# Second block: output transposes amid the branch product, heads ahead of the weight splits, gate sigmoids grouped, and a second pair of filling banks

## The chip, the cores and the metric

The kernel runs on one core of one Trainium2 chip. The metric is the device time of one execution in microseconds; lower is better. The engines named below are TensorE (PE in the profile: matmuls and transposes), VectorE (DVE), ScalarE (ACT), GpSimd (POOL) and SyncE (SP, which issues nearly all DMAs). All of them run at once, each through its own instruction stream in order, and they wait for one another on semaphores.

## The reference, cut to what matters

A first block (a hybrid of a state-space mixer and attention, a mixture of experts, a gated side input) is followed by a second one on the same 256 rows of 1024 numbers. The change touches the second block only:

```python
h = rms_norm_2(x, g_norm)
proj = h @ w_in
hy_in, z_hy, c_q, c_kv, k_rope, z_attn, gate_hy, gate_attn = split(proj)
u = short_conv(hy_in, w_short, b_short);  v_h, x1, x2 = split(u, 3)
zc = v_h
for o, gate in enumerate((x1, x2)):              # two rounds through spectra
    zc = gate * long_conv(zc, k_spec[:, o], hy_bias[o])
u_hy = (zc * silu(z_hy)) @ w_hy_out              # "branch", weights whn
q, k, v_a = ...                                  # from c_q, c_kv, k_rope: 8 heads
attn = dense_bidirectional_attention(q, k, v_a)
u_attn = (attn * silu(z_attn)) @ w_attn_out      # weights wa2
g_hy, g_at = split(sigmoid(concat([gate_hy, gate_attn]) + b_gate))
x = x + (g_hy * u_hy + g_at * u_attn) @ w_out    # weights wo2
```

## The kernel before

**Large products.** Every float32 weight is cut by columns and rows into tiles of at most 128x2048 numbers (four chunks of 128 rows by 512 columns). A tile passes through three stations: SP fetches it into one of four raw buffers; ACT writes its rounded high part (`weights` in `scalar`, L1209: `WH<-raw`); DVE writes the rest (`weights` in `vector`, L1705: `WL<-raw,WH`). High and low parts live in three slots, so a tile can be split only when the tile three before it has been used up by PE. The activations are split in the same way after their transposes: `high` on ACT (L1227) and `low` on DVE (L1735). A chunk of a product is then three matmuls for each half of the rows (`mul3`, L500), six in all, into two PSUM banks.

**Order of the tiles at the end.** The columns of z_attn ("za", two tiles), four gate groups (`("gate", 0)` to `("gate", 3)`, two tiles each), `whn` 0 and 1 (one tile each), `wa2` 0 and 1 (one each), `wo2` 0 and 1 (two each, called a and b below). 0 and 1 are the left and right 512 output columns.

**Filling.** The products that nobody needs at once are a list of single chunks, `todo`. Each engine's code calls `fill(n)` at the same places, which takes the next n chunks: PE multiplies; ACT and DVE (`filled`) split the weights that have come due and, behind a product's last chunk, take the product out of PSUM. za is taken out by ACT with a Silu, the gates by DVE with scale and bias (L1758), and then ACT applies the Sigmoid in place (L1271). The branch products (`whn` 0 and 1) are multiplied by the gates on DVE (L1766).

**PSUM banks.** `Ring` hands out the eight banks. `take` returns the next one of `ring.of` and first makes PE wait until the bank's former content has been taken out (its "drainer"). In the spectral stage `ring.of` is banks 0 to 5, and every filling product sits in banks 6 and 7.

**The stage with the spectra** (PE from 673.98 us on, `for o_ in range(2)` in `tensor`): two rounds of four forward products (`uf`, plain float32 from the arena), fillings (9 chunks in the first round, 4 and 3 in the second), two inverse products (`ui`), and more fillings (4 and 2). The eight za chunks and the sixteen of gates 0 and 1 are filled in here. Just ahead of it stand the products of the latents, `kq` and `kv`; the last bank of `kv` is taken out by ACT (L1618 and L1620).

**The stage with the heads** (PE from 739.02 us to 791 us): eleven steps. Each may hold a head's transposes (L509 from the arena), a chunk of filling, the scores of the head before, another chunk, the transposes of the exponentials (L509 from XN), and the product with the values, which is collected in banks 4 and 5. On ACT a step holds the copies of the transposed head (L1661, L1662), the exponentials (L1670), and for odd steps a copy of the weights (L1241); on DVE the row maxima (L2533, L2536) and for even steps that copy (L1745). Of the 24 filling chunks (gate 2, gate 3, branch 0, branch 1), 20 are used in the steps and the four of branch 1 behind them.

**The end.** DVE divides the heads' output by the sums and multiplies by silu(z_attn) (L2551, L2554, L2558, twice), PE transposes it (`transposed("o2T", ...)`, L509 from rt_), ACT and DVE split it, and `wa2` 0 and 1, the merge with the gates (L2566, L2569) and `wo2` 0 and 1 follow. The last step is `residual` on DVE (L2068) and the stores.

Of the kernel before, what the change touches and what calls it, by code (L numbers as in the profile page):

```python
# [14 lines left out]
ACT = mybir.ActivationFunctionType  # L15
# [150 lines left out]
def program(nc, A, out):  # L166
    ctx = ExitStack()
    with ctx:
# [326 lines left out]
        def tensor(e):  # L495
# [31 lines left out]

            open_fill = {}

            def fill(n):  # L530
                for name, c in todo.next(n):
                    key, lhs, ready, drainer, turned = fill_of[name]
                    if c == 0:
                        open_fill[name] = [ring.take((name, t), drainer, at=6 + t) for t in range(2)]
                    gemm_chunk(name, key, c, open_fill[name], lhs, ready, turned)
# [542 lines left out]
            todo.add(("gate", 0), 8)  # L1078
            todo.add(("gate", 1), 8)
            for o_ in range(2):  # L1080
                for f in range(2):
# [34 lines left out]
            todo.add(("branch", 1), 4)  # L1116
            ring.of = range(4)
            held_o2 = [ring.take(("o2", t), ve, at=4 + t) for t in range(2)]
# [34 lines left out]
            for h in range(11):  # L1153
# [9 lines left out]
                if h >= 3:  # L1163
                    values2(h - 3)
            fill(99)
            ring.of, ring.i = range(8), 0


            ve.wait_ge(e, "o2")
            transposed("o2T", lambda t: O2[:, t, :], 4)  # L1170
            gemm(("wa2", 0), ("wa2", 0), OT2, "o2T", (ve, ve))
# [24 lines left out]
        def scalar(e):  # L1196
# [42 lines left out]
            def drain_t(name, dst):  # L1239
                mm.wait_ge(e, name)  # L1240
                e.activation(dst, pb(name)[:, 0:dst.shape[1]], ACT.Copy).then_inc(ac.sem, ac.mark(name))  # L1241

            def filled(name, c):
                key = fill_of[name][0]
# [20 lines left out]
                elif name == "za":  # L1265
                    drain(name, ZA, ACT.Silu, by=rg)
                elif name[0] == "gate":
                    for t in range(2):
                        gv = G_[i // 2][:, t, (i % 2) * 512:(i % 2) * 512 + 512]
                        ve.wait_ge(e, (name, t))  # L1270
                        e.activation(gv, gv, ACT.Sigmoid).then_inc(ac.sem, ac.mark((name, t)))  # L1271
                weights(used(key))
# [402 lines left out]
            for h in range(11):  # L1675
# [7 lines left out]
                if 2 <= h <= 9 and h % 2:  # L1683
                    if h >= 6:
                        mm.wait_ge(e, ("pv2", h - 6))
                    drain_t(("p2", h - 2), P2[(h - 2) % 4])
            fill(99)
            high("o2T", OT2, 4, after=(("gate", 3), 1))
            weights(used(("wa2", 0)))
# [7 lines left out]
        def vector(e):  # L1697
# [48 lines left out]

            def filled(name, c):
                key = fill_of[name][0]
# [11 lines left out]
                elif name[0] == "branch":  # L1760
                    i = name[1]
                    ac.wait_ge(e, (("gate", i), 1))
                    for t in range(2):
                        gv = G1[:, t, 512 * i:512 * i + 512]
                        mm.wait_ge(e, (name, t))
                        e.tensor_tensor(gv, pb((name, t))[:, :], gv, ALU.mult).then_inc(ve.sem, ve.mark((name, t)))  # L1766
                weights(used(key))

            def fill(n):
                for name, c in todo.next(n):  # L1770
                    filled(name, c)

# [765 lines left out]
            for h in range(11):  # L2538
                fill(1)
                if 1 <= h <= 8:  # L2540
# [8 lines left out]
            for t in range(2):  # L2549
# [7 lines left out]
                ve.wait_ge(e, ("o2", t))  # L2557
                e.tensor_tensor(O2[:, t, :], O2[:, t, :], ZA[:, t, :], ALU.mult).then_inc(ve.sem, own("o2"))  # L2558
            fill(99)
            low("o2T", OT2, 4)  # L2560
            for i in range(2):
# [12 lines left out]
            low("m2T", HT, 8, first=4)  # L2574
            weights(used(("wa2", 1)))
            ac.wait_ge(e, "x 1")
            for i in range(2):
                residual(("wo2", i), i, ("x 2", i))
                weights(used(("wo2", i)))

# [159 lines left out]
```

## Time and profile before

| | us |
|---|---|
| median of 3 runs | 846.97 (846.54 to 847.56) |
| the profiled execution, its own time | 844.72 |
| its span from first to last instruction | 842.9 |
| PE busy in the span | 760.5 (90%) |
| DVE busy | 459.2 (54%) |
| ACT busy | 325.0 (39%) |

The span is what the views of the trace count in; 1.8 us lie around it. The median of the timed runs is 2.25 us above the profiled execution's own time. A row of the timeline gives the start, the duration and, in brackets, how long the engine had been idle before it and which instruction of which engine released it. Starts of neighbouring matmuls are more telling than durations, since matmuls overlap in the pipeline.

### The profile page before, as it was taken

To read this page: it belongs to the slowest core of one execution; us is meant where nothing else is said; L and a number is where in the kernel's file an instruction comes from. 1 tells how busy PE (TensorE), PEld (TensorE's weight loads), DVE (VectorE), ACT (ScalarE), POOL (GpSimd) and SP (SyncE) were. 2 spreads that over 40 slices of the span, in tenths; PEclk is the share of its full clock that TensorE was granted. 3 is DMA by queue.
4 is the path that set the end of the run, shared out by engine and by line. 5 is a ranking of instruction groups with operands and counts; after the bars stand their busy time and mean duration, and the time that the engine had idled before them with its cause. 6 is when DMAs were issued, how large, how long until landed. Compare 5 with 4: busy or idle time off the path is not lost.

```text
span 842.9 us, 11017 instructions
## 1 busy us (share of the span) xinstructions
PE 760.5 (90%) x4618; PEld 573.6 (68%) x4618; DVE 459.2 (54%) x813; ACT 325.0 (39%) x482; POOL 17.8 (2%) x14
## 2 busy tenths in 40 slices
PE   4999999999999997988799896779999999999898
PEld 4978877788778875555445542337999865678676
DVE  5778955547756755132142121028687786754653
ACT  5555446535464423111011010037755541267521
POOL 0000000000000000000000000001100020000000
PEclk9999999999999997999899898789999999999999
DMA  9555543333467596699999999875463734243301
GB/s 317 172 199 199 200 150 101 100 101 101 149 244 277 191 425 260 213 422 420 421 421 420 419 422 391 338 265 185 146 228 94 255 130 149 101 150 100 100 1 51
DMA packets 62578, 190.25 MB, mean 226 GB/s; under 512 B 7417, under 2 KB 11771, under 8 KB 50044
## 3 DMA queue, kind: packets, MB, share of 16 engines
q1 hardware_dynamic: 60750, 184.70, 58.6%
q10 hardware_dynamic: 1774, 4.79, 1.8%
q8 instruction: 38, 0.62, 0.3%
q14 instruction: 16, 0.13, 0.0%
HBM read 188.43 MB, written 1.05 MB: 225 GB/s over the span
## 4 chain that ended last, share of the span: by engine, by line
PE 59%; DMA 16%; DVE 13%; ACT 8%; issue 2%; POOL 1%; SPq 0%; ACTq 0%; DVEq 0%; POOLq 0%
PE pb L500 56%; DMA raw<-in_w_exp_up 7%; DVE WL L1705 4%; DMA WHo<-in_w_exp_up 4%; ACT WH L1209 4%; PE pb L509 3%; DMA WLo<-in_w_exp_up 3%; DMA raw<-in_w_exp_gate 2%; ACT arena L1365 1%; DMA X<-in_x 1%; DVE cv_ L1811 1%; DVE arena L1970 1%; POOL small L2587 1%; ACT arena L1237 0%; DVE arena L2016 0%
## 5 line engine op out<-in xcount | busy, mean ns | idle before, releaser
L1705 DVE TENSOR_TENSOR WL<-raw,WH 128x2048 fp32r<-128x2048 f32 (+5 forms) x80 | 173.4, 2177 | 98.2 <-ACT WH L1209 98.1
L1209 ACT ACTIVATE WH<-raw 128x2048 fp32r<-128x2048 f32 (+5 forms) x80 | 144.9, 1822 | 99.4 <-PE pb L500 89.9
L500 PE MATMUL pb<-WH,HTh 128*128 128x512 f32 (+2 forms) x384 | 156.0, 406 | 13.6 <-DVE HTl L1735 3.4
L500 PE MATMUL pb<-WL,HTh 128*128 128x512 f32 (+2 forms) x384 | 148.3, 386 | 0.0
L500 PE MATMUL pb<-WH,HTl 128*128 128x512 f32 (+2 forms) x384 | 148.0, 386 | 0.0
L500 PEld LDWEIGHTS pb<-WH,HTh 128*128 128x128 f32 x384 | 72.7, 189 | 33.7 <-DVE WL L1705 6.4
L500 PEld LDWEIGHTS pb<-WL,HTh 128*128 128x128 f32 x384 | 72.5, 189 | 14.4
L500 PEld LDWEIGHTS pb<-WH,HTl 128*128 128x128 f32 x384 | 72.8, 190 | 12.9 <-issue 1.0
L500 PE MATMUL pb<-arena 128*32 128x256 f32 (+6 forms) x268 | 64.0, 466 | 7.4 <-DMA arena<-in_w_exp_up 4.8
L500 PE MATMUL pb<-WH,arenao 128*128 128x512 f32 x192 | 59.6, 392 | 1.2 <-DVE arenao L1739 1.2
L2244 DVE TENSOR_TENSOR rt_<-rt_,pb 128x256 f32<-128x256 f32 x8 | 3.4, 421 | 98.9 <-ACT rt_ L1480 98.9
L500 PE MATMUL pb<-HTh,WH 128*128 128x256 f32 (+1 forms) x184 | 52.9, 287 | 0.1
L500 PE MATMUL pb<-HTh,WL 128*128 128x256 f32 (+1 forms) x184 | 52.4, 285 | 0.0
L500 PE MATMUL pb<-HTl,WH 128*128 128x256 f32 (+1 forms) x184 | 52.4, 285 | 0.0
L500 PE MATMUL pb<-raw,arena 128*32 128x256 f32 x272 | 37.7, 496 | 13.6 <-DMA raw<-in_w_exp_gate 6.9
L500 PEld LDWEIGHTS pb<-arena 128*32 128x32 f32 (+4 forms) x268 | 29.5, 168 | 28.2 <-issue 10.4
L1480 ACT ACTIVATE rt_<-pb 128x256 f32<-128x256 f32 x8 | 3.1, 383 | 105.3 <-PE pb L500 105.3
L500 PEld LDWEIGHTS pb<-WH,arenao 128*128 128x128 f32 x192 | 35.7, 188 | 8.6 <-DVE WL L1705 1.4
L500 PE MATMUL pb<-XN,arena 128*128 128x64 f32 (+2 forms) x144 | 37.9, 418 | 0.8 <-DVE arena L2016 0.8
L500 PE MATMUL pb<-WL,arenao 128*128 128x512 f32 x96 | 37.5, 390 | 0.0
L500 PEld LDWEIGHTS pb<-raw,arena 128*32 128x32 f32 x272 | 16.6, 141 | 28.5 <-DMA raw<-in_w_exp_gate 9.3
L500 PEld LDWEIGHTS pb<-HTh,WH 128*128 128x128 f32 (+1 forms) x184 | 35.0, 190 | 0.8 <-DVE WL L1705 0.5
(360 smaller groups left out, 1287.4 us busy)
## 6 DMA issues: line engine op xcount, KB each, us to landing
raw<-in_w_in SPq DMA_DIRECT2D x46, 1024.0 KB, 5.1
raw<-in_w_exp_up SPq DMA_DIRECT2D x16, 1024.0 KB, 21.3
arena<-in_w_exp_gate SPq DMA_DIRECT2D x14, 1024.0 KB, 19.1
WLo<-in_w_exp_down SPq DMA_DIRECT2D x11, 1024.0 KB, 17.0
raw<-in_w_exp_gate SPq DMA_DIRECT2D x10, 1024.0 KB, 14.8
WHo<-in_w_exp_down SPq DMA_DIRECT2D x9, 1024.0 KB, 16.5
raw<-in_w_out SPq DMA_DIRECT2D x8, 1024.0 KB, 5.1
arena<-in_w_exp_down SPq DMA_DIRECT2D x8, 1024.0 KB, 16.0
```

The source lines that it names most:

```text
L500: return e.matmul(o, l, r, start=start, stop=stop, skip_group_check=True)
L509: return e.transpose(o, i, ident[0:k, 0:k])
L1209: e.activation(h_, r_, ACT.Copy).then_inc(hi.sem, hi.mark(k))
L1365: ins = e.activation(S1[s][:, cut], S1[s][:, cut], ACT.Exp, bias=nmx[:, s, t:t + 1], scale=-1.0, accum_out=ssum[:, t, h:h + 1])
L1480: e.activation(HG[q % 2], pb(("gu", q))[:, 0:256], ACT.Silu).then_inc(ac.sem, ac.mark(("su", q)))
L1705: e.tensor_tensor(l_, r_, h_.bitcast(F32), ALU.subtract).then_inc(lo.sem, lo.mark(k))
L1811: e.scalar_tensor_tensor(out=cv[:, s:L], in0=u[:, 0:L - s], scalar=cw[:, 3 - s, g:g + 1], in1=cv[:, s:L], op0=ALU.mult, op1=ALU.add).then_inc(
L1970: ins = e.scalar_tensor_tensor(out=LM[:, h, :], in0=pb(("lm", t, h0))[:, (h - h0) * 128:(h - h0) * 128 + 128], scalar=Ac[:, t, h:h + 1], i ...
L2244: e.tensor_tensor(HG[q % 2], HG[q % 2], pb(("gu", q))[:, 256:512], ALU.mult).then_inc(ve.sem, ve.mark(("gu", q)))
L2587: e.tensor_tensor(ss, ss, half, ALU.pow).then_inc(po.sem, po.mark(("rs", n)))
```

## The change

Five edits, all in the second block:

1. In the spectral stage `ring.of` becomes banks 0 to 3, begun again at bank 0. The filling products alternate between banks 6 and 7 and banks 4 and 5. Behind the stage they are back at 6 and 7 alone.
2. ACT applies the sigmoid of gates 2 and 3 behind the last step of the heads, no longer behind each gate's last chunk, and splits `o2T` ahead of the last filling.
3. PE waits for the heads' output and transposes it behind the second of branch 1's four chunks, no longer behind the fourth.
4. DVE leaves out the split that comes due behind branch 0's last chunk until the heads' output is normalised, and writes the low part of `o2T` ahead of the last filling.
5. DVE splits the last tile (`wo2` 1 b) ahead of the residual of the left columns.

```diff
@@ tensor
-            open_fill = {}
+            open_fill, fill_at = {}, deque([6])
                     if c == 0:
-                        open_fill[name] = [ring.take((name, t), drainer, at=6 + t) for t in range(2)]
+                        open_fill[name] = [ring.take((name, t), drainer, at=fill_at[0] + t) for t in range(2)]
+                        fill_at.rotate(1)
...
             todo.add(("gate", 1), 8)
+            ring.of, ring.i = range(4), 0
+            fill_at.append(4)
             for o_ in range(2):
...
             todo.add(("branch", 1), 4)
-            ring.of = range(4)
+            fill_at.clear()
+            fill_at.append(6)
...
                 if h >= 3:
                     values2(h - 3)
+            fill(2)
+            ve.wait_ge(e, "o2")
+            transposed("o2T", lambda t: O2[:, t, :], 4)
             fill(99)
             ring.of, ring.i = range(8), 0
-            ve.wait_ge(e, "o2")
-            transposed("o2T", lambda t: O2[:, t, :], 4)
             gemm(("wa2", 0), ("wa2", 0), OT2, "o2T", (ve, ve))
@@ scalar
+            def sigmoid(i):
+                for t in range(2):
+                    gv = G_[i // 2][:, t, (i % 2) * 512:(i % 2) * 512 + 512]
+                    ve.wait_ge(e, (("gate", i), t))
+                    e.activation(gv, gv, ACT.Sigmoid).then_inc(ac.sem, ac.mark((("gate", i), t)))
...
-                elif name[0] == "gate":
-                    for t in range(2):
-                        gv = G_[i // 2][:, t, (i % 2) * 512:(i % 2) * 512 + 512]
-                        ve.wait_ge(e, (name, t))
-                        e.activation(gv, gv, ACT.Sigmoid).then_inc(ac.sem, ac.mark((name, t)))
+                elif name[0] == "gate" and i < 2:
+                    sigmoid(i)
                 weights(used(key))
...
+            for i in (2, 3):
+                sigmoid(i)
+            high("o2T", OT2, 4, after=(("gate", 3), 1))
             fill(99)
-            high("o2T", OT2, 4, after=(("gate", 3), 1))
             weights(used(("wa2", 0)))
@@ vector
-            def filled(name, c):
+            def filled(name, c, split):
...
-                weights(used(key))
-            def fill(n):
+                if split:
+                    weights(used(key))
+            def fill(n, split=True):
                 for name, c in todo.next(n):
-                    filled(name, c)
+                    filled(name, c, split)
...
             for h in range(11):
-                fill(1)
+                fill(1, h < 10)
...
                 e.tensor_tensor(O2[:, t, :], O2[:, t, :], ZA[:, t, :], ALU.mult).then_inc(ve.sem, own("o2"))
+            weights(used(("whn", 0)))
+            low("o2T", OT2, 4)
             fill(99)
-            low("o2T", OT2, 4)
...
             weights(used(("wa2", 1)))
+            weights(used(("wo2", 0)))
             ac.wait_ge(e, "x 1")
             for i in range(2):
                 residual(("wo2", i), i, ("x 2", i))
-                weights(used(("wo2", i)))
```

PE at the start of the spectral stage, before the change. The rows with arena are the first-round `uf` products, `pb` with its number is the bank, `[waits s_ac]` a wait for ACT, `s_ve` for DVE, `s_lo` for DVE's weight splits:

```order
L500 MATMUL pb0<-WL,HDh 128x512
L500 MATMUL pb1<-arena 128x512 [waits s_ve]
L500 MATMUL pb1<-arena 128x512
L500 MATMUL pb2<-arena 128x512 [waits s_ac]
L500 MATMUL pb2<-arena 128x512
```

The same place with the change:

```order
L500 MATMUL pb0<-WL,HDh 128x512
L500 MATMUL pb0<-arena 128x512 [waits s_ac]
L500 MATMUL pb0<-arena 128x512
L500 MATMUL pb1<-arena 128x512 [waits s_ve]
L500 MATMUL pb1<-arena 128x512
```

The first `uf` product moved from bank 1 to bank 0, the bank in which the last `kv` product has just ended, and its wait from DVE to ACT.

DVE from the product of branch 0 (the first row) to the end of the first merge's preparation, before. `rt_` is the heads' output, `WL<-raw,WH` a weight split, `HTl` the low part of `o2T`:

```order
L1766 TENSOR_TENSOR arena<-pb,arena 128x512 x2
L1705 TENSOR_TENSOR WL<-raw,WH 128x2048
L2551 RECIPROCAL small<-small 128x8
L2554 TENSOR_TENSOR rt_<-pb,small 128x512
L2558 TENSOR_TENSOR rt_<-rt_ 128x512
L2551 RECIPROCAL small<-small 128x8
L2554 TENSOR_TENSOR rt_<-pb,small 128x512
L2558 TENSOR_TENSOR rt_<-rt_ 128x512
L1766 TENSOR_TENSOR arena<-pb,arena 128x512 x2
L1705 TENSOR_TENSOR WL<-raw,WH 128x2048
L1735 TENSOR_TENSOR HTl<-pb,HTh 128x512 x2
```

The same with the change (its line numbers are 10 to 11 higher):

```order
L1776 TENSOR_TENSOR arena<-pb,arena 128x512 x2
L2562 RECIPROCAL small<-small 128x8
L2565 TENSOR_TENSOR rt_<-pb,small 128x512
L2569 TENSOR_TENSOR rt_<-rt_ 128x512
L2562 RECIPROCAL small<-small 128x8
L2565 TENSOR_TENSOR rt_<-pb,small 128x512
L2569 TENSOR_TENSOR rt_<-rt_ 128x512
L1715 TENSOR_TENSOR WL<-raw,WH 128x2048
L1745 TENSOR_TENSOR HTl<-pb,HTh 128x512 x2
L1776 TENSOR_TENSOR arena<-pb,arena 128x512 x2
L1715 TENSOR_TENSOR WL<-raw,WH 128x2048
```

The first split moved behind the heads' output; the low part of `o2T` moved ahead of branch 1's product and of the second split.

ACT from the last copy of a head on, before (`XN` are exponentials, `sg_` and `cv_` copies of the weights of the heads, `arena<-arena` sigmoids):

```order
L1670 ACTIVATE XN,small<-pb,small 128x256 x2
L1271 ACT_TABLE_LOAD
L1271 ACTIVATE arena<-arena 128x512 x2
L1209 ACTIVATE WH<-raw 128x2048
L1241 ACTIVATE sg_<-pb 128x512
L1670 ACT_TABLE_LOAD
L1670 ACTIVATE XN,small<-pb,small 128x256 x2
L1241 ACTIVATE cv_<-pb 128x512
L1209 ACTIVATE WH<-raw 128x2048 x2
L1227 ACTIVATE HTh<-pb 128x512 x2
```

And with the change:

```order
L1678 ACTIVATE XN,small<-pb,small 128x256 x2
L1214 ACTIVATE WH<-raw 128x2048
L1246 ACTIVATE sg_<-pb 128x512
L1678 ACTIVATE XN,small<-pb,small 128x256 x2
L1246 ACTIVATE cv_<-pb 128x512
L1214 ACTIVATE WH<-raw 128x2048
L1252 ACT_TABLE_LOAD
L1252 ACTIVATE arena<-arena 128x512 x4
L1232 ACTIVATE HTh<-pb 128x512 x2
L1214 ACTIVATE WH<-raw 128x2048 x2
```

Two table loads and two sigmoids went from between the exponentials (two more loads went with gate 2's, earlier), four sigmoids and one load came ahead of `HTh`, and one split moved behind it.

## Rows read from the trace of the kernel before

**Rows 1.** Page, part 1: busy time of PE, share of the span, instructions.

```profile
PE 760.5 (90%) x4618; PEld 573.6 (68%) x4618; DVE 459.2 (54%) x813; ACT 325.0 (39%) x482; POOL 17.8 (2%) x14
```

**Rows 2.** Waits of PE, 670 to 843 us: total us, times, longest.

```profile
PE pb L500 <- DVE HTl L1735: 3.4, 1, 3.4
PE pb L500 <- DVE arena L1758: 3.0, 3, 1.6
PE pb L500 <- ACT rt_ L1237: 1.7, 1, 1.7
PE pb L509 <- ACT XN L1670: 1.3, 1, 1.3
PE pb L500 <- DVE WL L1705: 0.9, 1, 0.9
```

**Rows 3.** Timeline of PE, spectral stage: start, us, instructions, idle before.

```profile
673.98 7.03 PE L500 MATMUL pb<-arena 128*128 128x512 f32 x16
680.44 0.79 PE L500 MATMUL pb<-WH,HTh 128*128 128x512 f32 x1
...
691.28 0.39 PE L500 MATMUL pb<-WH,HTl 128*128 128x512 f32 x1
691.51 0.39 PE L500 MATMUL pb<-WL,HTh 128*128 128x512 f32 x1
693.60 0.47 PE L500 MATMUL pb<-WH,HTh 128*128 128x512 f32 x1 [1.70 <-ACT rt_ L1237]
...
720.12 0.47 PE L500 MATMUL pb<-WH,HTh 128*128 128x512 f32 x1 [1.62 <-DVE arena L1758]
```

**Rows 4.** Timeline of ACT: last drain of `kv`, gate 3's sigmoids, last two splits.

```profile
676.31 0.38 ACT L1620 ACTIVATE arena<-pb 128x256 f32<-128x256 f32 x1
...
778.74 1.28 ACT L1271 ACT_TABLE_LOAD   x1
780.03 1.15 ACT L1271 ACTIVATE arena<-arena 128x512 f32<-128x512 f32 x2
781.09 1.90 ACT L1209 ACTIVATE WH<-raw 128x2048 fp32r<-128x2048 f32 x1
...
821.47 3.72 ACT L1209 ACTIVATE WH<-raw 128x2048 fp32r<-128x2048 f32 x2
```

**Rows 5.** Timeline of PE, last heads and the end.

```profile
787.40 0.66 PE L509 MATMUL pb<-c,XN 128*128 128x128 f32 x4 [1.30 <-ACT XN L1670]
...
802.57 0.77 PE L500 MATMUL pb<-WH,HTh 128*128 128x512 f32 x1 [3.41 <-DVE HTl L1735]
...
805.27 0.44 PE L500 MATMUL pb<-WH,HTh 128*128 128x512 f32 x1
...
831.30 0.50 PE L500 MATMUL pb<-WH,HTh 128*128 128x512 f32 x1 [0.86 <-DVE WL L1705]
```

**Rows 6.** Timeline of DVE, branch 0's product to the low part of `o2T`.

```profile
790.38 1.29 DVE L1766 TENSOR_TENSOR arena<-pb,arena 128x512 f32<-128x512 f32 x2 [3.67 <-PE pb L500]
...
794.59 0.20 DVE L2551 RECIPROCAL small<-small 128x8 f32<-128x8 f32 x1
...
797.18 0.69 DVE L2558 TENSOR_TENSOR rt_<-rt_ 128x512 f32<-128x512 f32 x1
...
799.53 2.29 DVE L1705 TENSOR_TENSOR WL<-raw,WH 128x2048 fp32r<-128x2048 f32 x1 [0.46 <-ACT WH L1209]
801.74 1.28 DVE L1735 TENSOR_TENSOR HTl<-pb,HTh 128x512 fp32r<-128x512 f32 x2
```

**Rows 7.** Timeline of PE, two idle stretches elsewhere in the kernel.

```profile
168.78 0.47 PE L500 MATMUL pb<-WH,HTh 128*128 128x512 f32 x1 [2.02 <-ACT arena L1237]
...
325.28 0.58 PE L500 MATMUL pb<-cv_o,HTh 128*128 128x256 f32 x1 [2.82 <-DVE HTl L2085]
```

**Rows 8.** Stretches of 1 us: busy PE, PEld, DVE, ACT, POOL, granted clock, DMA share, GB/s.

```profile
324.00:325.00 1.00, 0.00 (x0) 0.00 (x0) 1.00 (x1) 0.00 (x0) 0.00 (x0) 0.54 0.98 410
802.00:803.00 1.00, 0.43 (x1) 0.46 (x2) 1.00 (x2) 0.00 (x0) 0.00 (x0) 0.50 0.00 0
```

## The prediction, made before the changed kernel was run

> **What bounds the kernel now.** First the page: PE is busy 90% of the span [rows 1], so time is won only where PE stands still or runs slowly. Then the view of who waits for whom, cut to PE from 670 us on [rows 2]: some 10.3 us of idling, and each row names a target of the change. The longest, 3.4 us, is the wait of the first `wa2` matmul for the low part of the transposed heads. Then three waits of together 3.0 us for the drain of a gate: one filling product waits until the former one has left banks 6 and 7. The same at the drain of za, 1.7 us. Then 1.3 us for the last exponentials and 0.9 us for the last weight split. Last the timelines, for what stands in front of each releaser on its own engine. I work in the old trace's clock and carry the shift along.
>
> **Spectral stage, four banks for the filling.** Before, the last za matmul starts at 691.51 and gate 0's first at 693.60. Neighbours start 0.23 us apart (691.28 and 691.51), so without the wait for za's drain it would start at 691.74: 1.86 us are won [rows 3]. Gate 0 is followed by gate 1 with an idle time of 1.62 us at 720.12, about 1.8 us in starts [rows 3]; gate 1 goes to the banks of za, emptied long before, so this goes too. The third change, gate 1 to gate 2 (the last part of the 3.0 us in [rows 2]), stays: gate 1 sits in banks 6 and 7 and gate 2 is sent there again. That makes 3.66 us.
>
> The price is at the stage's start. The main ring is begun again at bank 0, which the last `kv` product has filled just before. ACT has emptied it at 676.31 + 0.38 = 676.69 [rows 4]; the release takes about 0.1 us. PE started its first `uf` product at 673.98 in bank 1, with no wait [rows 3]; now it starts at 676.79: 2.81 us lost. Is PE covered there by something later? Behind `uf` stand eight za chunks, which wait for nothing, and they started right behind `uf` at 680.44 [rows 3]; so the whole delay passes on. DVE's work on the first `uf` products, for which `ui` waits, has nine chunks (12.4 us) of PE's time to be done in, and DVE was still draining `kv` while the first products ran, so it is hardly late. Behind it DVE's products with `ui` come some 2.5 us later, and four gate chunks, 24 x 0.23 = 5.5 us, stand between them and the next `uf`. Net: 3.66 - 2.81 = 0.85 us gained. The first matmul behind a wait also costs 0.1 us more than one in a row, so I take **0.95 us**. Bounds: 0.5 us if one of the two drains is replaced by another wait, 3.7 us if ACT's drain of `kv` is not in the way.
>
> **Last exponentials.** ACT had, between the exponentials of heads 6 and 7, a table load of 1.28 us, two sigmoids of 1.15 us (780.03), the split at 781.09 and another table load [rows 4]. Without load and sigmoids the split begins at 778.75, 2.3 us earlier, DVE's low part and the row maximum behind it move with it, and the exponentials end near 785.1 instead of 787.35. PE wants them at 787.40 - 1.30 and a tenth, 786.0 [rows 5]. So the wait goes, 0.9 us of slack remain: **1.4 us** gained (bounds 1.2 and 1.5). The loads that go with gate 2's sigmoids lie in time in which PE does not wait: nothing.
>
> **Heads, transposes, low part.** All times here include the 1.4 us. DVE ends branch 0's product at 790.38 + 1.29 - 1.4 = 790.27 [rows 6]. The six instructions on the heads' output took from 794.59 to 797.87 [rows 6], 3.28 us; they now follow at once and end at 793.55. PE starts branch 1 a tenth later, at 790.37 (that wait for the banks of branch 0 stays), does two chunks, 12 matmuls of 0.23 us, until 793.2, idles 0.4 us for the heads, transposes from 793.62 (0.8 us in starts), does the other two chunks and is ready for `wa2` at **797.3**. Is the low part there? ACT: the split of `wa2` 1 waits for the end of branch 0's matmuls and ends near 791.0; table load 1.28 and four sigmoids of 0.53 us [rows 4] end at 794.4; the two high parts until 795.5. DVE: the split of `wa2` 1 behind the heads, 2.21 us, until 795.76; low parts until 796.4 and 797.0 (both durations from [rows 6]). The first chunk needs only the first. So 0.8 us of slack, and `wa2` starts at 797.3 instead of 802.57 [rows 5]: 5.27 us, of which 1.4 are counted: **3.87 us**. The transposes' banks 2 and 3 are empty by then. Who waits behind the moved work: DVE's product with branch 1 and its split for `wo2` 0 a end near 801.5, and PE needs that tile some 12 us after `wa2` starts; the merge finds DVE free at 802.8. The stalled wait on PE holds back only the last two branch chunks, and those are not needed before the merge. Bounds: 3.0 us if the high or low part comes up to 0.9 us late, 4.3 us if the 0.4 us of idling vanish.
>
> **Clock.** Behind the 3.41 us of idling PE is granted half its clock, 0.50 of 2.4 GHz, that is 1.2 GHz, in the row from 802 us on [rows 8]. Six matmuls took from 802.57 to 805.27, 2.70 us [rows 5]; at full clock they take 6 x 0.23 = 1.38 us. With the idling gone the low clock goes: **1.3 us** (bounds 0 and 1.4).
>
> **Last split.** `wo2` 1 b is split by DVE behind the residual and holds PE for 0.86 us before 831.30, 1.02 us in starts with the slow first matmul [rows 5]. ACT had both high parts of `wo2` 1 ready at 821.47 + 3.72 = 825.2 [rows 4], the first of them at half of that time; DVE now splits one right behind the other, 2.21 us each from about 823.4 on, until 827.9, and PE needs the last at 831.30 - 1.02 = 830.3. The left residual is hardly later for it, and its store is long over at the end. **1.0 us** (bounds 0.9 and 1.1).
>
> **Sum.** 0.95 + 1.4 + 3.87 + 1.3 + 1.0 = 8.5 us. Against the profiled execution: span 842.9 to 834.4, own time 844.72 to 836.2. The median lies 2.25 us above that execution's time and I keep the distance: 846.97 - 8.5 = **838.5 us**, a ratio of 0.990.
>
> **Rivals.**
> (A) *The new stall takes the clock down.* The stall of 2.8 us at 674 is new. For it speaks that the clock fell in the idling of 2.82 us before 325.28 [rows 7, 8]; against it, that idling there had other pauses ahead of it, that 2.02 us before 168.78 left the clock up [rows 7], and that at 802 it took nearly the whole 3.4 us. Price: 1.3 us as at 802.57; at most some 2.7 us, if the low stretch is twice as long. Result 839.8 to 841.2, say 840.3. Nothing later swallows it, since PE bounds this stage. The Trainium skill, "TensorE: Matmul & The Clock Gate", section "A second HAM failure mode: psum-queue depth-cycling", tells of a kernel that cycled through PSUM banks and idled between groups of matmuls so often that its clock went down and up again; by that, more turning of banks is a danger by itself. Here the rows are of two minds: the shorter pauses of 1.6 and 1.7 us at the bank changes left no low stretch, only the length of the new one is in doubt.
>
> (B) *The end turns its wait into another one.* The split of `wa2` 1 still stands ahead of the low part on DVE, and four sigmoids ahead of the high part on ACT. If either chain is 0.8 us later than worked out, PE waits; a full split more (2.2 us) gives 840.7, half of it 839.6. For it speaks that the slack is small; against it, that all durations are the trace's own.
>
> (C) *The stall at 674 does not come*, because bank 0 is empty sooner than I read. Then 838.5 - 2.8 = 835.7. The order of the instructions speaks against it: the first `uf` product has a wait for ACT that it did not have.
>
> (D) *Slower.* The mechanism of (A), but the clock stays at 1.2 GHz through the fillings. A matmul of 512 columns then starts every 0.43 us (2.70 us less the first one's extra, over six) instead of 0.23, 0.2 us more each. To eat 8.5 us and 1.7 more it must cover 51 matmuls, over 20 us in a row; from there on the kernel is slower than 848.7. At 802.57 the clock was back after 2.7 us of steady matmuls.
>
> (E) *Nothing.* The gain is given back by a wait that I don't see, say a late fetch of a `wo2` tile, whose raw buffer is freed by the split that edit 4 moves back. That split moves by about a microsecond only, and some 8 us would have to be lost. Result 847.
>
> **How the numbers follow.** Forecast 838.5: 0.60. (A) 0.17, (B) 0.13, (C) 0.04, (D) 0.03, (E) 0.03. The forecast's own bounds are 837.2 and 839.6. The range takes in (A) and (B): 837.0 to 841.8. A measurement of this kernel can tell about 0.2% (1.7 us) from no change: faster by more than that 0.94, within it 0.03, slower 0.03.
>
> **What would show it.** In the profile of the changed kernel: a wait of PE of about 2.6 us for ACT's drain of `kv` (the line of L1620) at 674 to 677, and a granted clock of 1.00 there; no wait for za's drain and one instead of three of over 1 us for the gates' drains; no wait for the last exponentials; a wait of 0.4 us for the heads' output ahead of the transposes, and under 0.3 us ahead of the first `wa2` matmul, with the clock at 1.00 behind it; no wait for the last split. Wrong it would be if the first `wa2` matmul waited over 1 us, if the clock fell at 677, or if the new stall shifted DVE's work in the first round so far that `ui` waits.

## The result, and the profile after

| | before | changed |
|---|---|---|
| median of the timed runs, us | 847.13 (846.54 to 847.56, 4 runs) | 835.32 (832.51 to 838.23, 4 runs) |
| ratio, 95% interval | | 0.9861 [0.9827, 0.9896] |
| profiled execution: own time / span, us | 844.72 / 842.9 | 838.23 / 836.3 |

The changed kernel takes 1.4% less time. (The kernel before stands at 847.13 us here because a fourth timed run has joined the three of 846.97.) Forecast were 838.5 us and a range that began at 837.0. The range missed the median by 1.7 us, on the fast side, while the single execution in the profile, at 838.23, lies almost on the forecast. That second agreement is luck, as the cut through the traces below shows: this execution lost 2.24 us in a part of the kernel that the change does not touch.

First the steps. The waits of PE in the second block (changed kernel, 672 to 837 us; total us, times, longest):

```profile
PE pb L500 <- ACT arena L1628: 2.6, 1, 2.6
PE pb L500 <- DVE arena L1768: 1.4, 2, 1.1
PE pb L500 <- DVE small L2562: 0.6, 1, 0.6
PE pb L500 <- DVE arena L1755: 0.2, 1, 0.2
PE pb L509 <- DVE rt_ L2569: 0.2, 1, 0.2
```

Set beside [rows 2]: the 3.4 us at the low part, the 1.7 us at za's drain, the longest of the three waits for the gates' drains (1.62 of 3.0 us), the 1.3 us at the exponentials and the 0.9 us at the last split are gone. New is the first row, the stall for ACT's drain of `kv`. The timeline of PE in the changed kernel (start, us, instructions, idle before) gives their places:

```profile
679.01 7.13 PE L500 MATMUL pb<-arena 128*128 128x512 f32 x16 [2.61 <-ACT arena L1628]
...
742.04 0.47 PE L500 MATMUL pb<-WH,HTh 128*128 128x512 f32 x1 [1.11 <-DVE arena L1768]
...
787.25 0.60 PE L509 MATMUL pb<-c,XN 128*128 128x128 f32 x4
...
791.56 0.47 PE L500 MATMUL pb<-WH,HDh 128*128 128x512 f32 x1 [0.59 <-DVE small L2562]
...
794.71 1.23 PE L509 MATMUL pb<-c,rt_ 128*128 128x128 f32 x8 [0.19 <-DVE rt_ L2569]
...
798.53 0.39 PE L500 MATMUL pb<-WH,HTh 128*128 128x512 f32 x1
```

(The releaser in the fourth row, `small L2562`, is the instruction that DVE did next; what PE waited for is the product of branch 0 just ahead of it, as before the change.) The last row is the first `wa2` matmul. It has no wait and is of full speed at once (0.39 us against 0.77 in [rows 5]). In the timeline of ACT, ACT has emptied bank 0 at 678.58 + 0.38 = 678.96, and PE starts at 679.01. ACT comes to this so late because it makes a weight split of 1.91 us first, the first row. The exponentials of head 7 and the four sigmoids behind them stand there too:

```profile
676.50 1.91 ACT L1214 ACTIVATE WH<-raw 128x2048 fp32r<-128x2048 f32 x1 [0.81 <-PE pb L500]
...
678.58 0.38 ACT L1628 ACTIVATE arena<-pb 128x256 f32<-128x256 f32 x1
...
785.00 0.56 ACT L1678 ACTIVATE XN<-pb,small 128x256 f32<-128x256 f32 x1 [2.67 <-DVE small L2547]
...
793.73 2.19 ACT L1252 ACTIVATE arena<-arena 128x512 f32<-128x512 f32 x4
```

The timeline of DVE has the heads' output ahead of the split, the low part right behind that, and the two last splits in one row:

```profile
793.97 0.69 DVE L2569 TENSOR_TENSOR rt_<-rt_ 128x512 f32<-128x512 f32 x1
794.58 2.28 DVE L1715 TENSOR_TENSOR WL<-raw,WH 128x2048 fp32r<-128x2048 f32 x1
796.78 1.28 DVE L1745 TENSOR_TENSOR HTl<-pb,HTh 128x512 fp32r<-128x512 f32 x2
...
817.96 4.49 DVE L1715 TENSOR_TENSOR WL<-raw,WH 128x2048 fp32r<-128x2048 f32 x2 [1.00 <-ACT WH L1214]
```

The low part ends at 796.78 + 1.28 = 798.06, 0.47 us ahead of the first `wa2` matmul. The granted clock behind the new stall and at the start of `wa2` (stretches of the changed kernel: length, busy PE, PEld, DVE, ACT, POOL, clock, DMA share, GB/s):

```profile
676.00:680.00 4.00, 1.39 (x5) 0.51 (x4) 3.70 (x4) 2.46 (x3) 0.00 (x0) 1.00 0.93 290
797.00:800.00 3.00, 3.00 (x15) 2.49 (x14) 2.33 (x4) 1.21 (x1) 0.00 (x0) 1.00 0.59 173
```

**A cut through the traces.** All of this happens behind 667 us. To compare it apart from what goes before, I cut each trace at one matmul, the first of the `kv` products, behind a wait of 0.68 us for DVE, which lies ahead of everything that the change touches ("the first kv matmul" in the expectations). Before, the rows are, with two others that are used below:

```profile
230.98 2.00 PE L500 MATMUL pb<-XN,arena 128*128 128x64 f32 x16 [0.77 <-DVE arena L2016]
...
252.12 2.04 PE L509 MATMUL pb<-c,XN 128*128 128x128 f32 x16 [1.54 <-DVE XN L2033]
...
667.88 0.50 PE L500 MATMUL pb<-WH,HDh 128*128 128x512 f32 x1 [0.68 <-DVE arena L1745]
```

and the same three in the changed kernel:

```profile
231.96 2.00 PE L500 MATMUL pb<-XN,arena 128*128 128x64 f32 x16 [0.78 <-DVE arena L2027]
...
256.33 2.04 PE L509 MATMUL pb<-c,XN 128*128 128x128 f32 x16 [1.55 <-DVE XN L2044]
...
670.12 0.50 PE L500 MATMUL pb<-WH,HDh 128*128 128x512 f32 x1 [0.68 <-DVE arena L1755]
```

The part ahead, in which both kernels have the same instructions, took 667.88 and 670.12 us: the changed kernel lost 2.24 us where nothing was changed. The part behind (span less this start) took 842.9 - 667.88 = 175.02 and 836.3 - 670.12 = 166.18 us: 8.84 us won. Spans are known to 0.1 us, so a part behind is known to some 0.05 us. The experiments are read by these two parts.

### The profile page after: what moved, and what is told of

Read it like the earlier page. It is cut to its first block, busy times and chain, and to the rows that moved or that the text cites. A ratio compares the mean times of both kernels' runs of the same rounds, so it can differ in the third digit from the quotient of the medians.

```text
span 836.3 us, 11015 instructions
## 1 busy us (share of the span) xinstructions
PE 761.8 (91%) x4618; PEld 574.4 (69%) x4618; DVE 459.3 (55%) x813; ACT 321.2 (38%) x479; POOL 17.8 (2%) x14
## 4 chain that ended last, share of the span: by engine, by line
PE 65%; DMA 14%; DVE 11%; ACT 7%; issue 2%; POOL 1%; SPq 0%; ACTq 0%; DVEq 0%; POOLq 0%
PE pb L500 61%; DMA raw<-in_w_exp_up 7%; DMA WHo<-in_w_exp_up 4%; PE pb L509 4%; DVE WL L1715 4%; ACT WH L1214 3%; DMA raw<-in_w_exp_gate 2%; ACT arena L1373 1%; DVE cv_ L1822 1%; DMA X<-in_x 1%; DVE arena L1981 1%; POOL small L2599 1%; ACT arena L1242 0%; DVE arena L2027 0%; ACT arena L1408 0%
```

## The experiments

My theory after the result: the sum of 8.5 us is right term by term for the part behind, and the forecast missed because the part ahead differs from one execution to the next, so that the distance of the first profiled execution from the median told nothing. The rival: the change gains something that I did not count, about 3 us, in the block or elsewhere.

**The same two kernels again.** No edit.

> The kernel before, unchanged, for a second trace and more times. Theory 1 (the edits gave what was summed, and the rest of the median's gain is a clock that falls by chance in stages nobody touched): the part from the first kv matmul to the end is 175.0 us as in the first trace, within 0.3 us, unless a low clock shows in it; the part ahead of it differs from the first trace's 667.9 us by up to 4 us, and every such difference lies in stretches with a granted clock below 1.00. Theory 2 (the end itself takes different times): the 175.0 us differ and the part ahead doesn't.

> The changed kernel, unchanged, for a second trace and more times. Theory 1: from the first kv matmul to the end 166.2 us as in its first trace, within 0.3 us, with the times of whole executions spread over several us by low clocks ahead of it. Theory 2 (in most executions the changed part is some 3 us shorter than in the profiled one): 163 us in the second trace.

| | median, us (runs) | ratio, 95% | span | part ahead | part behind |
|---|---|---|---|---|---|
| before, again | 847.37 (12) | 1.0012 [0.9998, 1.0026] | 845.7 | 670.66 | 175.04 |
| changed, again | 836.39 (6) | 0.9886 [0.9864, 0.9908] | 836.7 | 670.59 | 166.11 |

The ratios are against 23 runs of the kernel before on the same chip, median 846.53 (844.35 to 852.01). This pair happens to have the same part ahead within 0.1 us, so its spans can be compared directly: 845.7 - 836.7 = 9.0 us. The part behind came back within 0.1 us for either kernel, and the part ahead of the unchanged kernel moved by 2.8 us. Own times of unchanged code thus range over some microseconds: single runs of the kernel before went from 844.68 to 848.76.

**The edits in two groups.** `banks_only` is the kernel before with edit 1 alone; `tail_only` is the changed kernel without edit 1:

```diff
-            ring.of, ring.i = range(4), 0
-            fill_at.append(4)
...
-            fill_at.clear()
-            fill_at.append(6)
+            ring.of = range(4)
```

> Edit 1 alone. By the prediction's sum 0.95 us less than before from the first kv matmul to the end (174.0 us): minus 3.66 us of drain waits, plus 2.81 us of stall for ACT at the first uf product. The median falls by 1 us, or by 1 to 4 us if low clocks behind the removed pauses cost time in other executions.

> Edits 2 to 5 without the banks (edit 1): the spectral stage is as before, banks 0 to 5 and 6, 7. By the prediction's sum 7.6 us less than before in the part from the first kv matmul to the end (167.4 us), about 1 us more than the whole change, and no stall for ACT at the first uf product. Rival (the bank edit carries more than was summed, since the pauses of 1.7 us that it removes sometimes bring the clock down): the median is 3 us or more above the whole change's.

| | median, us (runs) | ratio, 95% | span | part ahead | part behind |
|---|---|---|---|---|---|
| `banks_only` | 842.78 (12) | 0.9966 [0.9946, 0.9985] | 840.4 | 666.03 | 174.37 |
| `tail_only` | 837.45 (6) | 0.9904 [0.9886, 0.9923] | 837.4 | 670.23 | 167.17 |

The waits of PE from 670 us on in `banks_only`:

```profile
PE pb L500 <- DVE HTl L1739: 3.4, 1, 3.4
PE pb L500 <- ACT arena L1624: 2.6, 1, 2.6
PE pb L500 <- DVE arena L1762: 1.4, 2, 1.1
```

and in `tail_only` (671 to 838 us):

```profile
PE pb L500 <- DVE arena L1765: 3.0, 3, 1.6
PE pb L500 <- ACT rt_ L1239: 1.7, 1, 1.7
```

In the first the waits of the end have stayed and the stall of 2.6 us has come; in the second the drain waits have stayed and the stall is absent. Edit 1 is worth 167.17 - 166.18 = 0.99 us in the part behind (0.95 forecast), and edits 2 to 5 are worth 175.02 - 167.17 = 7.85 (1.4 + 3.87 + 1.3 + 1.0 = 7.57 forecast). `banks_only` shows only 175.02 - 174.37 = 0.65 us for edit 1. Its low clock behind the wait of 3.4 us began just after PE's restart and lay wholly on matmuls:

```profile
799.76 0.57 PE L500 MATMUL pb<-WH,HTh 128*128 128x512 f32 x1 [3.40 <-DVE HTl L1739]
...
803.48 0.40 PE L500 MATMUL pb<-WH,HTh 128*128 128x512 f32 x1
```

Between these two starts lie 9 matmuls in 3.72 us, where 9 x 0.23 = 2.07 us would do at full clock. The low clock cost 1.6 us here against 1.3 us in the first execution of the kernel before, and that 0.3 us hides a part of edit 1.

The medians bear on the rival. `tail_only` should have been 3 us or more above the changed kernel; it is 837.45 - 836.39 = 1.06 us above it, so there the rival did not come. `banks_only` lies 846.53 - 842.78 = 3.75 us under the kernel before, which is more than the 1 us of the sum and within the 1 to 4 us that the rival allowed. This comes back under "Open".

**Taking the stall away.** If the stall comes only from the ring's beginning in the bank that `kv` has just filled, beginning one bank further must save all 2.8 us:

```diff
-            ring.of, ring.i = range(4), 0
+            ring.of, ring.i = range(4), 1
```

> The whole change, but the main ring of the spectral stage begins at bank 1, so that bank 0 with the last kv product comes fourth. If the stall of 2.6 us for ACT's drain costs its full length, the part from the first kv matmul to the end falls from 166.15 us to 163.4 us (2.61 us and the slow first matmul). Rival: PE then waits elsewhere in the stage, because DVE's products and the drain of za don't come earlier; the part falls by less than 1.5 us.

Median 832.67 us (4 runs), ratio 0.9845 [0.9815, 0.9876]; span 829.4, part ahead 666.11, part behind **163.29**, that is 2.89 us less than in the changed kernel. The waits of PE from 670 us on:

```profile
PE pb L500 <- DVE arena L1768: 1.4, 2, 1.1
PE pb L500 <- DVE small L2562: 0.6, 1, 0.6
PE pb L509 <- DVE rt_ L2569: 0.2, 1, 0.2
```

The stall has gone and nothing has come in its place. The span, 829.4 us, is 6.9 us under the changed kernel's, but 4.0 of them are the part ahead.

**Keeping four banks through the third drain.** The wait of 1.11 us between gate 1 and gate 2 comes from the filling's going back to two banks. `o2_high` is `start_bank1` with the filling in banks 4 and 5 during the heads, and the heads' output in 6 and 7, taken when they are free:

```diff
-            fill_at.append(6)
-            held_o2 = [ring.take(("o2", t), ve, at=4 + t) for t in range(2)]
+            fill_at.append(4)
+            ring.i, held_o2 = 14, []
...
+                if h == 3:
+                    held_o2[:] = [ring.take(("o2", t), ve, at=6 + t) for t in range(2)]
```

> As start_bank1, and in the stage of the heads the filling sits in banks 4 and 5 and the heads' output in 6 and 7, taken only ahead of the third step, so that gate 2 doesn't wait for gate 1's drain. Expected: the wait of 1.11 us (1.3 us in starts) goes too: 162.1 us for the part, 4 us less than the whole change, and a median near 832. Rival: DVE's or ACT's work sets that stage's pace and takes the gain back; 163.4 us as start_bank1.

Median 831.97 us (829.9 to 834.03, 5 runs), ratio 0.982 [0.9793, 0.9846]; span 830.8, part ahead 668.85, part behind **161.95**. The waits:

```profile
PE pb L500 <- DVE small L2564: 0.6, 1, 0.6
PE pb L500 <- DVE arena L1770: 0.3, 1, 0.3
PE pb L500 <- DVE arena L1757: 0.2, 1, 0.2
PE pb L509 <- DVE rt_ L2571: 0.2, 1, 0.2
```

Of the wait of 1.1 us nothing is left: 1.34 us less than `start_bank1`. This is the best version by the part behind, 4.2 us less than the changed kernel; its median can't be told from that of `start_bank1`, 832.67. By the ratios to the kernel before, its interval lies wholly below that of the changed kernel's second measurement and overlaps that of its first one by 0.0019.

**Undoing single edits of the end.** `sigmoids_amid` puts the sigmoids of gates 2 and 3 back behind their last chunks, `last_split_late` the last split behind the residual:

```diff
-                elif name[0] == "gate" and i < 2:
+                elif name[0] == "gate":
...
-            for i in (2, 3):
-                sigmoid(i)
```

```diff
-            weights(used(("wo2", 0)))
             ac.wait_ge(e, "x 1")
             for i in range(2):
                 residual(("wo2", i), i, ("x 2", i))
+                weights(used(("wo2", i)))
```

> The whole change with the sigmoids of gates 2 and 3 back behind each gate's last chunk. By the prediction the wait for the last exponentials comes back: 1.4 us more than the whole change's 166.15 us, 167.5 us, and nothing is won at the end by the shorter chain of ACT. Rival (the four sigmoids and the table load ahead of the high part hold the end up more than they save): 166.2 us or less.

> The whole change with the last split back behind the residual of the left columns (edit 5 undone). By the prediction 1.0 us more: 167.15 us, with a wait of 0.86 us for DVE's split ahead of the last product's fifth chunk.

Parts behind of 167.65 (span 836.1, ahead 668.45) and 167.28 us (span 833.7, ahead 666.42), so edit 2's sigmoids are worth 1.47 us and edit 5 is worth 1.10 (forecast 1.4 and 1.0). The wait that each brings back, from the waits of PE in `sigmoids_amid` and then in `last_split_late`:

```profile
PE pb L509 <- ACT XN L1678: 1.3, 1, 1.3
```

```profile
PE pb L500 <- DVE WL L1715: 0.9, 1, 0.9
```

What remains of the 7.85 us is 7.85 - 1.47 - 1.10 = 5.28 us for the heads, the transposes, the low part and the clock together (3.87 + 1.3 = 5.17 forecast).

**Undoing half of edit 4.** `split_ahead` lets DVE make the split behind branch 0 at once, ahead of the heads' output:

```diff
-                fill(1, h < 10)
+                fill(1)
...
-            weights(used(("whn", 0)))
```

> The whole change, but DVE does the split that comes due behind branch 0 at once, ahead of the heads' output (edit 4 undone in this half). By the prediction's working the transposes wait 2.2 us longer, nothing behind them is nearer to its limit, and the part from the first kv matmul on takes 168.3 us instead of 166.15 us. Rival (the wait for the heads has slack, since ACT's sigmoids bound the low part anyway): under 167 us.

Part behind **172.2** us (span 840.3, ahead 668.10). Both expectations, 168.3 and under 167, were missed by 4 to 5 us. The timeline of DVE shows a step that I had left out, a wait of the split itself for ACT's high part:

```profile
790.37 2.29 DVE L1715 TENSOR_TENSOR WL<-raw,WH 128x2048 fp32r<-128x2048 f32 x1 [0.99 <-ACT WH L1214]
792.58 0.20 DVE L2562 RECIPROCAL small<-small 128x8 f32<-128x8 f32 x1
```

So the heads' output is late by 0.99 + 2.21 = 3.2 us instead of 2.2, and PE idles for it ahead of the transposes:

```profile
795.92 1.98 PE L509 MATMUL pb<-c,rt_ 128*128 128x128 f32 x8 [3.47 <-DVE rt_ L2569]
```

Behind the longer wait the low clock is back (one trace). A stretch behind it:

```profile
798.00:801.00 3.00, 3.00 (x8) 2.32 (x8) 1.10 (x2) 0.54 (x1) 0.00 (x0) 0.50 0.00 0
```

PE runs at 1.2 GHz here, 8 matmuls in 3 us where 3 us at full clock hold 13. 172.2 - 166.18 = 6.0 us is 3.47 - 0.19 = 3.28 us of additional waiting and 2.7 us by which the low clock lengthens the work. The theory that edit 4 wins a split's length was right in kind. It was 2.2 us on paper and is 6.0 with what hangs on it.

**How much does a low clock cost, and how far does the part ahead move?** Three more executions of the kernel before, with no edit.

> The kernel before, once more, for a third trace. In two traces its part from the first kv matmul on took 175.0 us, and only the part ahead differed (667.9 and 670.7 us), by low clocks in other places. Theory 1 (chance of where the clock falls, the same for every kernel): again 175.0 us. Theory 3 (in some executions the pauses of 1.6 and 1.7 us at the filling's bank changes bring the clock down too, which no trace has caught; the change removes them, so it gains more in the median than in the traces): a low clock behind 693 or 720 us and 1 to 3 us more.

> The kernel before, for a fourth trace. In the third its part from the first kv matmul on took 176.6 us instead of 175.0 us: behind the wait of 3.4 us the clock stayed low for 6.8 us instead of 3.4 us. Theory 3a (only this low stretch varies): 175.0 or 176.6 us. Theory 3b (the pauses of 1.7 and 1.6 us near 693 and 720 us bring the clock down as well, in executions not yet caught): a low clock near 694 or 721 us and 1 to 3 us more. The means of the times ask for some 177 us.

> The kernel before, for a fifth trace, with the same two theories as for the fourth: 175.0 or 176.6 us by theory 3a, a low clock near 694 or 721 us by theory 3b.

| kernel before | own time | span | part ahead | part behind |
|---|---|---|---|---|
| first | 844.72 | 842.9 | 667.88 | 175.02 |
| again | 847.52 | 845.7 | 670.66 | 175.04 |
| third | 847.09 | 845.3 | 668.68 | **176.62** |
| fourth | 847.65 | 845.8 | 670.76 | 175.04 |
| fifth | 844.61 | 842.8 | 666.21 | **176.59** |

The part behind has two values, 1.6 us apart, and the clock behind the wait ahead of `wa2` tells them apart. In the third execution, the timeline of PE:

```profile
803.36 0.77 PE L500 MATMUL pb<-WH,HTh 128*128 128x512 f32 x1 [3.37 <-DVE HTl L1735]
803.92 0.63 PE L500 MATMUL pb<-WH,HTl 128*128 128x512 f32 x1
...
809.05 0.62 PE L500 MATMUL pb<-WH,HTl 128*128 128x512 f32 x1
809.47 0.43 PE L500 MATMUL pb<-WL,HTh 128*128 128x512 f32 x1
```

and a stretch of it, then the same stretch of the first execution:

```profile
804.00:807.00 3.00, 3.00 (x9) 2.33 (x8) 0.00 (x0) 0.00 (x0) 0.00 (x0) 0.50 0.03 5
```

```profile
804.00:807.00 3.00, 3.00 (x12) 2.41 (x11) 0.00 (x0) 0.00 (x0) 0.00 (x0) 0.77 0.03 5
```

Between the starts at 803.36 and 809.47 lie 14 matmuls in 6.11 us, where at full clock 14 x 0.23 = 3.22 us would do: the low clock cost 2.9 us. In the first execution it cost 1.3 us behind the same wait. Three executions of five have the cheap form, two the dear one; `banks_only`, with the same wait, lies between them at 1.6 us.

## Why the forecast was too high

**Right: what the edits do to the block.** In the clock of the trace before (the 2.24 us of the part ahead taken off), step by step:

| | forecast | found |
|---|---|---|
| first `uf` product, us | 676.79 | 676.77 |
| waits at za's drain, gate 0 to gate 1 | gone | gone |
| gate 1 to gate 2 | stays, start 739.78 | stays (1.11), start 739.80 |
| spectral stage | 0.95 | 0.99 |
| last exponentials | 1.4, no wait | 1.47, no wait |
| heads' output ahead of the transposes | wait 0.4, start 792.67 | wait 0.19, start 792.47 |
| first `wa2` matmul | 796.35, no wait | 796.29, no wait |
| heads to low part, with the clock | 5.17 | 5.28 |
| last split | 1.0 | 1.10 |
| sum, the part behind | 8.5 | 8.84 |

The forecasts for starts are the numbers of the prediction less the 0.95 us of the stage ahead, which it carried apart. The method, old times shifted by durations of the trace, held to 0.2 us or better for 120 us of program. The low part was complete 0.47 us ahead of its first use, where 0.3 was worked out, since the heads' output came 0.2 us sooner. One small reading was wrong: the three waits for the gates' drains were not all of over 1 us. Of their 3.0 us the first has 1.62 and the second 1.1, and the third 0.27 (at 779.49 us), so in the changed kernel two remain, 1.4 us in all.

**Wrong: the distance.** This is the step that failed. The prediction said that the median lies 2.25 us above that execution's time "and I keep the distance". It is no property of the kernel. Within one kernel the part ahead took between 666.21 and 670.76 us, over all 14 traces, in which its instructions are the same, between 666.03 and 670.76, 668.5 on average. The first execution of the kernel before was at 667.88, the changed kernel's at 670.12. With it the distance of median to profiled time went from +2.25 to 835.32 - 838.23 = -2.9 us. With the means measured since, the sum for the changed kernel is 668.5 ahead, 166.15 behind, and 1.9 us between span and own time, 836.5. Its 10 timed runs, medians 835.32 and 836.39, lie up to 1.2 us under that; the kernel before (668.5 + 175.7 + 1.8 = 846.0, against 847.13, 847.37 and 846.53) lies 0.5 to 1.4 us over it.

In numbers: forecast were 8.5 us between the medians, and they are 847.13 - 835.32 = 11.8 us apart. Of the missing 3.3 us, 0.34 us are in the terms as the first two traces show them (8.84) and 0.64 us in the clock term below (175.66 - 175.02). The remaining 2.3 us are in no trace. Medians of four runs that lie between 832.51 and 838.23 are too loose to carry them: the second measurement, with 6 and 23 runs, gave 846.53 - 836.39 = 10.1 us. So keeping the distance took the difference of one pair of executions for the difference of two medians of few runs, and the range, 1.5 us deep on the fast side, left no room for what that can be off.

**Mis-sized: the clock.** The step "1.3 us (bounds 0 and 1.4)" took the one low stretch of the one trace as all there is. In the kernel before the term measured 1.3 in three executions and 2.9 in two, 1.9 on average, and 1.6 in `banks_only`. The mean part behind over the five traces of the kernel before is 175.66 us, over the two of the changed kernel 166.15: the change is worth **9.5 us** on average, a ratio of 836.5/846.0 = 0.989, which lies inside the interval of either measurement. With bounds of 0 and 2.9 for this term and 2 us to either side for the part ahead the range would have begun near 835.

**The rivals.** (A), the stall takes the clock down, did not come: in the six traces that have the stall of 2.61 us (the changed kernel twice, `banks_only`, `sigmoids_amid`, `split_ahead`, `last_split_late`) the granted clock from 674 to 683 us is 1.00. (B), a wait at the end, did not come in the changed kernel, and `split_ahead` shows how near it was: one split more on the path of the heads cost 6.0 us. For that failure the price in (B), one split of 2.2 us, was too low, since the split waits for ACT and the low clock is back behind the new wait. (C) was made into `start_bank1` and is worth what was worked out, 2.9 us against 2.8. (D) and (E) did not come.

With rival (A) the prediction had read a danger in the turning of banks by itself. The section it named (the Trainium skill, "TensorE: Matmul & The Clock Gate", "A second HAM failure mode: psum-queue depth-cycling") tells of a kernel that cycles through PSUM banks and whose TensorE idles between groups of matmuls so often that its clock goes down and up. Here the turning came without the idling. From 680 to 698 us and from 715 to 723 us, where the filling of the changed kernel turns through four banks instead of two, PE is busy all the time (18.00 of 18 us and 8.00 of 8 us) and the clock stands at 1.00, and the version with most turning, `o2_high`, has the shortest part behind. So turning alone did no harm in these traces; frequent idling is not tested by them.

**Open.** The timed runs ask for somewhat more than the traces. Their means are 846.8 us for the kernel before and 836.0 for the changed one, 10.8 us apart against 9.5. Ten runs with a standard deviation of 2.2 us give a mean that is itself uncertain by some 0.7 us, so this may be chance. For `banks_only` chance is a weaker answer: its 12 runs have a mean 3.2 us under that of the 23 runs beside them, and the interval of its ratio reaches from 1.3 to 4.6 us, with the 0.99 us found for edit 1 just outside. A low stretch behind one of the old pauses of 1.6 or 1.7 us, which four banks remove, would explain it. Against this, no trace that has these pauses (six) shows one, and `tail_only`, which has the pauses, is only 1.06 us above the changed kernel. The cause stays open.

Two things were not run alone: edit 3, and the place of the low part in edit 4. Of the 5.28 us for the heads, the transposes, the low part and the clock, only the place of the split was tested. The clock's share is read from the old low stretches; no run keeps the wait and loses the low clock.

## What to carry to other kernels

Work a forecast out as a difference of parts, and cut both traces at an instruction ahead of the change before comparing spans; here that took a 4.7 us scatter out of a 9 us effect, and both parts behind came back within 0.1 us where the clock took the same form. A cost read from one low stretch of the clock is one draw; here the same wait cost 1.3 us or 2.9 us. Before trusting a median against one profiled execution, profile the kernel before a second and third time, and give the range room for the scatter of a median of few runs. When a ring of buffers is begun anew, don't begin it at the buffer that has just been filled: beginning at bank 0 instead of 1 cost 2.9 of the 167.17 - 163.29 = 3.9 us that the additional banks can win.

## What the runs showed of the hardware

**The same wait, with and without a low clock.** PE waits 2.02 to 2.04 us for ACT at 168 us in all 14 traces [rows 7]. The granted clock behind it is 1.00 in the first execution of the kernel before and in `split_ahead`, and falls in the other 12 traces. Stretches of the kernel before, at 168 and at 234 us:

```profile
168.00:171.00 3.00, 2.22 (x13) 1.94 (x14) 0.48 (x1) 2.49 (x3) 0.00 (x0) 1.00 0.00 0
...
234.00:237.00 3.00, 3.00 (x14) 2.50 (x14) 2.87 (x4) 0.00 (x0) 0.00 (x0) 1.00 0.00 0
```

The changed kernel:

```profile
168.00:171.00 3.00, 2.87 (x12) 2.42 (x13) 1.13 (x1) 1.84 (x2) 0.00 (x0) 0.71 0.00 0
...
234.00:237.00 3.00, 3.00 (x5) 1.31 (x6) 1.83 (x3) 0.00 (x0) 0.00 (x0) 0.52 0.00 0
237.00:240.00 3.00, 3.00 (x8) 2.32 (x8) 2.97 (x3) 0.00 (x0) 0.00 (x0) 0.50 0.00 0
```

From 234 to 243 us the clock fell in 5 of the 14 traces, and these are the five with a part ahead over 670 us (670.12 to 670.76; the other nine are at 668.85 or less). What it costs there can be read from the landmarks shown above: between the two matmul groups lie 252.12 - 230.98 = 21.14 us before and 256.33 - 231.96 = 24.37 us in the changed kernel, 3.2 us for the same instructions. In `before_again`, where the low stretch is shorter, they are 254.99 - 232.25 = 22.74 us apart, a cost of 1.6 us.

The other nine traces fall into a group at 666.0 to 666.4 us and one at 667.9 to 668.9 us. Most of that, too, is one low stretch. Between the matmul behind the idling of 2.82 us [rows 7] and the one behind an idling of 3.4 us near 375 us, the same instructions take 48.6 us in three of the first group and 49.6 us in its fourth, and 50.7 us in four of the second group and 49.6 us in its fifth. The granted clock is 0.55 from 334 to 337 us in the first execution of the kernel before (50.7 us) and 1.00 from 335 to 338 us, the same place, in `banks_only` (48.6 us).

**Longer idling is no surer to bring it.** Behind the stall of 2.61 us the clock never fell (0 of 6 traces), behind the one of 2.02 us it fell in 12 of 14, behind the one of 2.82 us near 325 us in all 14, behind the wait of 3.4 us ahead of `wa2` in all five traces of the kernel before, with 2.7 us of slow matmuls in three of them and 6.1 us in two. So the length of an idle stretch alone did not tell here whether the clock falls, nor what that costs. Rival (A), at 0.17, had been weighed mostly by lengths.
